# Route, mixers and expert retrieval on one core: score banks released after their first pass, part of the retrieval's search moved into the route, three operations moved to ScalarE

## The reference

```python
# HGRN2, per chunk:  S = exp(last) * S + einsum(kdec, v)
# RG-LRU:
a = exp(log_a)
b = sqrt(-expm1(2.0 * log_a)) * (i * xc)

# expert retrieval, for 8 heads, each with 2 halves of a query of 2 x 128:
q = (xb @ w_q).reshape(blk, PEER_HEADS, 2, PEER_DHALF)
s = einsum('thpc,hpnc->thpn', q, keys32)          # 128 scores a half
sv, si = top_k(s, 16)
cand = sv[:, :, 0, :, None] + sv[:, :, 1, None, :]  # 256 sums a head
cidx = si[:, :, 0, :, None] * 128 + si[:, :, 1, None, :]
cs, ci = top_k(cand, 16)
eidx = take_along_axis(cidx, ci);  g = softmax(cs)
act = gelu(einsum('thkd,td->thk', U[eidx], xb))
out = einsum('thk,thkd->td', g * act, V[eidx])
```

## Time and profile before

| what | value |
|---|---|
| runs | 3506.56, 3506.3, 3500.5 us; median 3506.3 |
| profiled execution | 3501.6 us; its span 3499.9 us |
| mean granted TensorE clock | 0.951 of full speed |
| mixers / route | about 343 to 576 / 722 to 987 us of the span |
| experts: first phase, dense loop | 987 to 1116, 1116 to 1521 us |
| experts: weight loop, last 16 steps | 1521 to 2056, 2056 to 2244 us |
| experts' outputs | from 2274 us |

### The profile page before, as it was taken

One profiled execution on the slowest core, in us unless ns is written; L12 is line 12 of the kernel. 1 busy time (PEld: TensorE's weight loads), 2 busy tenths in 40 slices (PEclk: granted clock), 3 DMA queues, 4 the chain that ended last, 5 costly groups with the idle time before them and its releaser, 6 DMA issues. The chain is left out here.

```text
span 3499.9 us, 51067 instructions
## 1 busy us (share of the span) xinstructions
PE 3196.2 (91%) x17340; PEld 2889.2 (83%) x17340; DVE 2718.1 (78%) x4921; ACT 1069.1 (31%) x1389; POOL 968.8 (28%) x796
## 2 busy tenths in 40 slices
PE   7998567889979999999999988889999999999988
PEld 6998345779979999999999987768888888888877
DVE  3000785278878999999999987579999999999954
ACT  3111553221122322235555531122222222222242
POOL 0000000000001555544444446333343334333300
PEclk9999677989989999999999999989999999999999
DMA  3222321011145999999999999799999999999821
GB/s 117 89 89 91 107 81 58 20 28 40 27 127 160 282 291 283 290 299 324 325 324 324 324 332 353 273 344 359 361 354 352 362 350 350 360 353 346 305 96 55
DMA packets 407543, 822.84 MB, mean 235 GB/s; under 512 B 40736, under 2 KB 257712, under 8 KB 400048
## 3 DMA queue, kind: packets, MB, share of 16 engines
q0 software_dynamic: 110592, 402.70, 34.2%
q1 hardware_dynamic: 274992, 318.60, 29.2%
q10 hardware_dynamic: 21888, 100.67, 7.3%
HBM read 696.74 MB, written 125.12 MB: 235 GB/s over the span
## 5 line engine op out<-in xcount | busy, mean ns | idle before, releaser
L260 PE MATMUL ea_pa<-rest_hi,ea_uhi 128*128 128x384 f32 x2048 | 705.5, 344 | 78.6 <-DVE ea_ulo L1481 76.2
L1205 POOL DMA_INDIRECT h<-in_peer_u,ga_rows x384 | 555.2, 1446 | 692.0 <-DVE ea_acc L1608 463.0
L262 PE MATMUL ea_pa<-rest_hi,ea_ulo 128*128 128x384 f32 x2048 | 693.0, 338 | 0.0
L261 PE MATMUL ea_pa<-rest_lo,ea_uhi 128*128 128x384 f32 x2048 | 692.9, 338 | 0.0
L1205 POOL DMA_INDIRECT eo_ring<-in_peer_v,ga_rows x384 | 406.6, 1059 | 682.9 <-DVE h L1894 627.6
L1894 DVE SCALAR_TENSOR_TENSOR h<-eo_ring,eo_share,h 128x1024 f32<-128x1024 f32 x384 | 490.5, 1278 | 0.0
L1608 DVE CUSTOM_DVE_ANT_0 h<-h,plain 128x1024 f32<-128x1024 f32 x384 | 454.0, 1218 | 36.6 <-DMA h<-in_peer_u,ga_rows 36.2
L260 PEld LDWEIGHTS ea_pa<-rest_hi,ea_uhi 128*128 128x128 f32 x2048 | 391.2, 191 | 88.9 <-issue 50.1
L261 PEld LDWEIGHTS ea_pa<-rest_lo,ea_uhi 128*128 128x128 f32 x2048 | 391.6, 191 | 0.0
L262 PEld LDWEIGHTS ea_pa<-rest_hi,ea_ulo 128*128 128x128 f32 x2048 | 390.8, 191 | 0.0
L1830 ACT ACTIVATE eo_phi<-eo_prod 128x512 fp32r<-128x512 f32 x192 | 121.6, 633 | 775.0 <-DVE eo_prod L1868 706.7
(11 more groups left out here) (320 smaller groups left out, 5964.8 us busy)
## 6 DMA issues: line engine op xcount, KB each, us to landing
ea_raw<-in_peer_u SPq DMA_DIRECT2D x512, 128.0 KB, 6.5
region<-in_peer_v SPq DMA_DIRECT2D x128, 512.0 KB, 11.1
act_scratch<-ea_stage ACTq DMA_DIRECT2D x128, 384.0 KB, 5.2
w_scratch<-region ACTq DMA_DIRECT2D x24, 2048.0 KB, 9.7
region<-w_scratch SPq DMA_DIRECT2D x16, 1536.0 KB, 13.8
region<-act_scratch SPq DMA_DIRECT2D x16, 1536.0 KB, 17.9
eo_wt<-w_scratch SPq DMA_DIRECT2D x16, 1536.0 KB, 13.8
eo_at<-act_scratch SPq DMA_DIRECT2D x16, 1536.0 KB, 17.9
```

The lines of the kernel that those rows point to most:

```text
L260: nc.tensor.matmul(out, w[0], x[0], start=first, stop=False)
L261: nc.tensor.matmul(out, w[0], x[1], start=False, stop=False)
L262: return nc.tensor.matmul(out, w[1], x[0], start=False, stop=last)
L1205: nc.gpsimd.indirect_dma_start(out=dst, out_offset=None, in_=table, in_offset=bass.IndirectOffsetOnAxis(ap=self.rows[:, m % GT, m // GT:m ...
```

## The change

1. **Mixers.** ACT makes `vmask` (eight Copies with a scale, right behind the `vtok` copy), copies `ps_kd` to `kdtok` and squares `r` into `cum`, both behind its Exp of `r`. A semaphore `a_squared` tells DVE of the square. DVE does `ig * xc` before `sf`.
2. **Route.** `scores_read` takes the place of `ranked`: it rises behind the first MAX, INDEX and REPLACE of all tiles, when the banks have been read. `lo` runs two halves ahead. `sums_of_head(i)` on DVE, behind the two ranks of a head, adds and searches that head's sums for the three gathered tiles, and copies 16 best sums and places to `ga.best` and `ga.at`.
3. **Experts, first phase.** `best_sums` and the searching half of `next_sums` are gone for the gathered tiles; `spread` (the copy of the indices) and `decode` (the rest of `next_sums`) read `ga.best` and `ga.at`. A tile takes two steps instead of four. Step 6 does `best_sums` of the first dense tile, and steps 6 to 11 take 2, 6, 6, 6, 6 and 6 dots (`DOTS_FIRST`, 32 in all). `DOTS_REST` comes out as 4 instead of 6. The dots' numbers in the later loops shift by 32. ACT's `exponentials` are called in other steps.

The diff, cut:

```diff
@@ mixers, ACT
                     f(vtok[:], ps_v, ACT.Copy).then_inc(v_tok, 1)
+                    e.wait_ge(v_tok, i + 1)
+                    for b in range(DB):
+                        last = f(vmask[:, b], vtok[:, NPT], ACT.Copy, scale=bmask[:, b:b + 1])
+                    last.then_inc(vmask_ready, 1)
...
                     f(r[:], r[:], ACT.Exp, scale=cur[:, NSP8:NSP8 + 1]).then_inc(exp_a, 1)
+                    e.wait_ge(kdec_t, i + 1)
+                    f(kdtok[:], ps_kd, ACT.Copy).then_inc(kdec_tok, 1)
+                    e.wait_ge(exp_a, i * 2 + 2)
+                    f(cum[:], r[:], ACT.Square).then_inc(a_squared, 1)
@@ mixers, DVE
-                    e.wait_ge(v_tok, i + 1)
-                    for b in range(DB):
-                        ins = v.tensor_scalar(vmask[:, b], vtok[:, NPT], bmask[:, b:b + 1], None, ALU.mult)
-                    ins.then_inc(vmask_ready, 1)
...
-                    e.wait_ge(kdec_t, i + 1)
-                    v.tensor_copy(kdtok[:], ps_kd).then_inc(kdec_tok, 1)
-
-                    e.wait_ge(exp_a, i * 2 + 2)
-                    link(v.tensor_tensor(cum[:], r[:], r[:], ALU.mult))
+                    e.wait_ge(sig_i, i + 1)
+                    o.did(v.tensor_tensor(ig[:], ig[:], xc, ALU.mult))
+                    e.wait_ge(a_squared, i + 1)
                     v.scalar_tensor_tensor(out=sf[:], in0=cum[:], scalar=1.0, in1=sf[:],
                                            op0=ALU.add, op1=ALU.mult).then_inc(va_ready, 1)
-                    e.wait_ge(sig_i, i + 1)
-                    link(v.tensor_tensor(ig[:], ig[:], xc, ALU.mult))
+                    o.settle()
@@ route, DVE
                         o.did(v.match_replace(rest[:, t], val[t][:, 0:8], scores[t], LOWEST))
                     wait_apart(e, P, o.sem, o.value())
+                    v.sem_inc(scores_read, 1)
...
+                def sums_of_head(i):
...
+                    for part in (slice(0, 8), slice(8, 16)):
+                        wait_apart(e, P, o.sem, o.value())
+                        for t in range(GT):
+                            o.did(v.max(sum16[:, t, part], cand[:, t]))
+                        wait_apart(e, P, o.sem, o.value())
+                        for t in range(GT):
+                            o.did(v.max_index(place16[:, t, part], sum16[:, t, part], cand[:, t]))
+                        if part.start == 0:
+                            wait_apart(e, P, o.sem, o.value())
+                            for t in range(GT):
+                                o.did(v.match_replace(cand[:, t], sum16[:, t, part], cand[:, t], LOWEST))
...
                 lo(0, 0)
+                lo(0, 1)
                 with e.Fori(0, LAST) as i:
-                    lo(i, 1)
+                    lo(i + 1, 0)
                     rank(i, 0)
-                    lo(i + 1, 0)
+                    lo(i + 1, 1)
                     rank(i, 1)
-                lo(LAST, 1)
+                    sums_of_head(i)
                 rank(LAST, 0)
                 rank(LAST, 1)
+                sums_of_head(LAST)
@@ route, PE
-                        e.wait_ge(ranked, n + 1)
+                        e.wait_ge(scores_read, n + 1)
@@ experts
+DOTS_FIRST = (0, 0, 0, 0, 0, 0, 2, 6, 6, 6, 6, 6)
...
-        DOTS_REST = (PICKS - DOTS_A - DOTS_W) // (4 * Q_REST)
+        DOTS_F = sum(DOTS_FIRST)
+        DOTS_REST = (PICKS - DOTS_F - DOTS_A - DOTS_W) // (4 * Q_REST)
...
-                    quad(i, lambda r: exponentials(i) if r == 1 else None)
+                    quad(i, lambda r: exponentials(2 * i + r // 2) if r % 2 == 0 and 2 * i + r // 2 < GT else None)
...
-                best_sums(first, 0)
-                for i in range(GT):
-                    split(*at_block(i, 2), lambda: next_sums(first, i))
-                    split(*at_block(i, 3), lambda: subkey(first, 0))
-                    split(*at_block(i, 4), lambda: subkey(first, 1))
-                    split(*at_block(i, 5), lambda: keep_chosen(first, i))
-                    best_sums(first, i + 1)
+                def first_step(j):
+                    i = j // 2
+                    if j < 2 * GT and j % 2 == 0:
+                        spread(first, i)
+                        decode(first, ga.best[:, i], ga.at[:, i])
+                        subkey(first, 0)
+                    elif j < 2 * GT:
+                        subkey(first, 1)
+                        keep_chosen(first, i)
+                    elif j == 2 * GT:
+                        best_sums(first, GT)
+                    for m in range(sum(DOTS_FIRST[:j]), sum(DOTS_FIRST[:j + 1])):
+                        dot(m, m % RING, m // RING, ga.dots[:, m:m + 1])
+
+                for j in range(4 * GT):
+                    split(*at_block(j // 4, j % 4 + 2), lambda: first_step(j))
```

More of the change, by code:

```diff
@@ L601, in mixers @@
              "st", "sn", "att_sum", "att", "qdz", "o_sum", "o_sq", "ms", "rms_root", "on", "on_t",
-             "state_t", "old", "sf_used", "e3_used", "xc", "silu_g", "gates", "va", "sqrt_b", "gelu_y", "oc", "oc_t", "rows", "self"))
+             "state_t", "old", "a_squared", "sf_used", "e3_used", "xc", "silu_g", "gates", "va", "sqrt_b", "gelu_y", "oc", "oc_t", "rows", "self"))
         NSTORE = 6
@@ L1055, in route_scores @@
         scores = [psc[:, t // 4, t % 4] for t in range(NT)]
-        hi_done, lo_done, q_sum, q_ready, k_t, kt_ready, scored, ranked, self_ok = map(
-            s, ("hi", "lo", "q_sum", "q_ready", "k_t", "kt", "scored", "ranked", "self"))
+        hi_done, lo_done, q_sum, q_ready, k_t, kt_ready, scored, scores_read, self_ok, sums_ok = map(
+            s, ("hi", "lo", "q_sum", "q_ready", "k_t", "kt", "scored", "scores_read", "self", "sums"))
         LAST = HP // 2 - 1
@@ L1130, in rank @@
                     o.settle()
-                    v.tensor_copy(si[:, :, bass.ds(n, 1), :].rearrange("p t a n -> p t (a n)"), ind16[:]
-                                  ).then_inc(ranked, 1)
+                    o.did(v.tensor_copy(si[:, :, bass.ds(n, 1), :].rearrange("p t a n -> p t (a n)"), ind16[:]))
+                    o.close()
+                def sums_of_head(i):
+                    o = Order(e, sums_ok, 5 * GT + 4, i)
+                    wide = NARROW * K
+                    half = lambda x: sv[:, 0:GT, bass.ds(i * 2 + x, 1), :].rearrange("p t a k -> p t (a k)")
+                    over = lambda x: x.rearrange("p t (k a) -> p t k a", a=1)
+                    under = lambda x: x.rearrange("p t (a k) -> p t a k", a=1)
+                    for of, first, second, shape in (
+                            (slice(0, wide), half(0)[:, :, 0:NARROW], half(1), [128, GT, NARROW, K]),
+                            (slice(wide, CANDS), half(0)[:, :, NARROW:K], half(1)[:, :, 0:NARROW],
+                             [128, GT, K - NARROW, NARROW])):
+                        o.did(v.tensor_tensor(cand[:, :, of].rearrange("p t (a b) -> p t a b", b=shape[3]),
+                                              over(first).broadcast_to(shape), under(second).broadcast_to(shape),
+                                              ALU.add))
+                    for part in (slice(0, 8), slice(8, 16)):
[9 more added lines that the diff above has]
+                                o.did(v.match_replace(cand[:, t], sum16[:, t, part], cand[:, t], LOWEST))
+                    o.settle()
+                    for dst, x in ((best, sum16), (at, place16)):
+                        o.did(v.tensor_copy(dst[:, :, bass.ds(i, 1), :].rearrange("p t a k -> p t (a k)"), x[:]))
+                    o.settle()
@@ L1310, in experts @@
         DOTS_A, DOTS_W = ND * PER_A, NSUB * DOTS_SUB
-        DOTS_REST = (PICKS - DOTS_A - DOTS_W) // (4 * Q_REST)
-        assert DOTS_A + DOTS_W + DOTS_REST * 4 * Q_REST == PICKS and sum(DOTS_BATCH) == DOTS_SUB
+        DOTS_F = sum(DOTS_FIRST)
+        DOTS_REST = (PICKS - DOTS_F - DOTS_A - DOTS_W) // (4 * Q_REST)
+        assert DOTS_F + DOTS_A + DOTS_W + DOTS_REST * 4 * Q_REST == PICKS and sum(DOTS_BATCH) == DOTS_SUB
         assert PER_A % RING == 0 and PER_W % RING == 0 and len(DOTS_STEP) == 4 * Q_DENSE
@@ L1491, in _, with spread @@
                 WIDE = NARROW * K
+                def spread(o, i):
+                    of_tile = si[:, bass.ds(i, 1)].rearrange("p a n k -> p (a n) k")
+                    o.did(v_.tensor_copy(
+                        sub.rearrange("p n (k t) -> p (n k) t", t=QUAD),
+                        of_tile.rearrange("p n (k a) -> p (n k) a", a=1).broadcast_to([128, HP * K, QUAD])))
                 def best_sums(o, i):
@@ L1620, in dots @@
                     for _ in range(counts):
-                        dot(m, m % RING, n * (per // RING) + (first + m) // RING, acc[:, m:m + 1])
+                        dot(first + m, (first + m) % RING, n * (per // RING) + (first + m) // RING, acc[:, m:m + 1])
                         m += 1
@@ L1651, in dense_picks @@
                             steps[r]()
```

(10 more changed lines are left out.)

26 lines of the change are left out of this document (16 added, 10 removed).

## The result

The changed kernel takes 3474.2 us (median of 4 runs, 3472.8 to 3482.8) against 3506.4 (4 runs, 3500.5 to 3509.2): ratio 0.9909, 95% interval 0.9893 to 0.9925, faster by 32 us. The forecast was 3475.

What follows compares the result with a forecast made beforehand. Bounds differed by stage: PE led the route, PE and DVE filled the dense loop, transfers paced the last 16 steps. From 3501.6 us, −4 + 14 + 6 − 44 = −28 gave 3473.6; adding 4.7, 3475 us, range 3456 to 3493.

Steps and rivals of the forecast that it cites:

- Mixers: Mixers stage: moving work from DVE to ACT shortens the chain to the states, −4 us, bounds −7 to +3.
- about 3.7: Mixers, iteration 1: the chain from the kdtok copy to states takes about 3.7 us instead of 5.32.
- iteration 2: Mixers, third iteration: ACT's late Exp of r eats most of the gain, leaving 0.2 us.
- Route: Route stage: the added sums make DVE the bound instead of PE, +14 us, bounds +10 to +20.
- 5.6: Route: DVE's added search of one head's sums for three tiles takes 5.6 us after each pair of ranks.
- 12.3: Route: one rank takes DVE 12.3 us, counted 16 times in the stage's sum.
- The split two ahead is costless so long as PE is not behind its weights: Route: making weight splits two halves ahead on DVE adds no cost unless PE is behind its weights.
- First phase: Experts' first phase: fewer searches but 32 dots added, with steps 8 to 11 gather-bound, +6 us, bounds −4 to +14.
- Last steps: Last 16 steps: four dots a step instead of six relieve the transfers, −44 us, bounds −54 to −38.
- I take 145: Last 16 steps: the stage takes 145 us, 9.05 a step.
- The slow rival: Route: PE's waits at the score banks lower its clock and the kernel becomes slower, about 3625 us; chance 0.04.
- The fast rival: First phase and last steps: transfers do not limit the steps that get the dots, about 3460 us; chance 0.13.

Runs made afterwards that it cites:

- e6: The changed kernel with the route's weight split one half ahead of the rank instead of two: 3508.0 us, ratio 1.0011 to the kernel before.
- e5: The changed kernel with the score banks released behind a rank's last copy instead of its first pass: 3495.3 us, ratio 0.9967 to the kernel before.
- e1: The changed kernel with no dots in the first phase and 6 a step at the end: 3504.4 us, ratio 0.9997 to the kernel before.
- e3: The changed kernel with 48 dots in the first phase and 3 a step at the end: 3487.2 us, ratio 0.9946 to the kernel before.
- e2: The changed kernel with 16 dots in the first phase and 5 a step at the end: 3478.0 us, ratio 0.9921 to the kernel before.
- e8: The changed kernel with the route's 16 weight splits on POOL instead of DVE: 3463.3 us, ratio 0.9878 to the kernel before.
- e7: The kernel before with only the early bank release and the splits two halves ahead, no sums in the route: 3507.5 us, ratio 1.0005.
- e10: The changed kernel as it is, run again for a second profile: 3474.8 us, ratio 0.9912 to the kernel before.

## Why the prediction was right, point by point

**The time.** 3475 forecast, 3474.2 measured, in the range and on the right side. The two large steps, a route bound by DVE and last steps freed of gathers, came as described; that the number fits to 1 us is luck. Four terms were each off by 2 to 7 us with signs that cancel, some us came in stages that the sum held at 0, and by the two profiles the stages sum to −18.9 and −24.6 where the forecast added up −28 and the medians of the runs differ by 32.3.

**Mixers**, −4: measured −5.6. The step "about 3.7" on the chain is 3.47. The mis-sized terms are iteration 0, put at 1.6, which gave about 2.3 (1.7 to 2.8 over the three profiles), and iteration 2, put at 0.2 with ACT's Exp as the cause, which gave 1.0.

**Route**, +14: measured +17.5, with the mechanism as described and DVE waiting once. The terms "5.6" for a head's sums (6.05 with the wait at the loop's end, 5.4 without it) and "12.3" for a rank (12.38) were small by 7 × 0.45 = 3.2 and 16 × 0.09 = 1.4. "The split two ahead is costless so long as PE is not behind its weights" is true as it stands, but it hid what the lead is for: with one half ahead the same route costs 34 us more (e6). The early release, to which the prediction gave no price of its own, is worth 21 (e5); PE's waits for banks past it are "at no cost while DVE sets the end", as it said.

**First phase**, +6: measured +9. "Steps 0 to 5 at about 8.55" were 8.96, all of it in the first, 10.98; step 7 was 10.5 instead of 9.8, and steps 8 to 11 were 12.1 instead of 11.5, transfers full at 342 GB/s.

**Last steps**, −44: measured −50. The cause (gathers) is shown by e1 to e3. The step "I take 145" added 3 us to the larger of two bounds, 142 by the transfers and 135 by PE, and the 142 came from 50 MB where 49.5 moved; the stage took 139.6 at 354 GB/s, with 136 of PE, so the bounds do not add. The Trainium skill's 425 GB/s for a 16 MB stream ("DMA: Bandwidth & Descriptors", section "Bandwidth") was not reached in the windows above whose share is 1.04 (334 to 355 GB/s). The same section's HBM figure of about 358 per core lies just above these means. It is no ceiling for shorter stretches here: slices of 3.5 us in the change's last steps have up to 417. What holds the mean is not shown.

**Dense and weight loops**, 0: +3.6 and +3.3 in the profiles of the change, but +1.9, +0.3 and −2.0 in e1, e2 and e3, +0.1 in e8. It is not a term of the change that these runs can show, and it was not followed further.

**The slow rival** (PE's clock in the route, 0.04) didn't come, but it was nearer than its chance. In two pairs of the changed kernel's route, at 848 and 914 us, PE's wait for the banks has grown to 2.74 us, and its products behind it slow down:

```profile
914.15 3.77 PE L1204 MATMUL rs_sc<-rs_kt,rs_q 128*128 128x128 f32 x18 [2.74 <-DVEq L1125]
```

against 2.27 elsewhere; the stretch 914.1 to 921 was granted 0.77. It costs nothing there: DVE is the bound, and its pairs stay at 33.1. The Trainium skill's rule on PSUM cycling ("TensorE: Matmul & The Clock Gate", section "A second HAM failure mode: psum-queue depth-cycling") is borne out in its direction by e5, where PE waits 3.1 to 3.8 us for the banks and the products behind are granted 0.50 to 0.56; in the route of before, with waits of 0.6 us and 0.98 granted, it did not apply. In e6 the same happens behind a wait for a weight split, which has nothing to do with banks.

**The fast rival** was half right: the last steps did reach nearly PE's pace (8.72 a step), the first phase did not reach DVE's.

## What to carry to other kernels

When a stage's pace is set by its transfers and another stage has idle ones, moving transfers pays until the second bound of each stage is met: 16 moved gathers were free, the next 16 paid 27 for 23, the third 16 paid 12 for 25. Work put on an engine with slack is dear from the point where the slack ends, so look next for a third engine that idles (here POOL, 11 us). And a hand-off that is worth nothing while one engine leads (e7) can be worth 21 to 34 us once the other leads (e5, e6): judge it in the kernel that it is part of.

## What the runs showed of the hardware that was not expected

A wait of PE of a few us can cost more than itself. Behind waits of 0.58 to 1.73 us the route's score products took 2.24 to 2.27 us in every profile. In the five profiles of this route (the change twice, e1 to e3) PE waits 2.72 to 2.76 us eleven times: behind ten of them the products took 3.2 to 3.9 us, at a granted 0.56 to 0.68, and behind one, in e10, they took 2.25 at 1.00:

```profile
912.67 2.25 PE L1204 MATMUL rs_sc<-rs_kt,rs_q 128*128 128x128 f32 x18 [2.73 <-DVEq L1125]
```

So a wait of that length puts the clock at risk and does not settle it. Behind the waits of 3.1 to 3.8 in e5 they took 3.87 to 4.18 every time, the longest at 0.50, PE's lower level of 1.2 GHz. And POOL's 128x1024 subtraction of 2.37 us left the ranks of DVE beside it at 12.4.
